# Expert jobs of a top-2-of-8 SwiGLU in plain float32: four column groups of 32 rows on TensorE, weights in rows of 6 and 8 KB in one ring

## The reference

```
def swiglu(x, w_gate, w_up, w_down):
    return (silu(x @ w_gate) * (x @ w_up)) @ w_down

def moe_swiglu(x, w_router, w_gate, w_up, w_down):     # x: 256 x 1024
    logits = xt @ w_router
    top_vals, top_idx = top_k(logits, 2)
    top_w = softmax(top_vals)
    gates = sum(one_hot(top_idx, 8) * top_w)
    for e in range(8):                                  # w_gate[e], w_up[e]: 1024 x 3584, w_down[e]: 3584 x 1024
        out = out + gates[:, e] * swiglu(xt, w_gate[e], w_up[e], w_down[e])
```

## Time and profile before

| what | value |
|---|---|
| time, median of 3 runs | 1460.51 us (1460.16 to 1460.75) |
| profiled execution, first to last instruction | 1458.9 us |
| median less that span | 1.6 us |
| first expert matmul | 495.2 us into the span |
| last expert matmul of weights | 1447.5 us |
| PE, DVE, ACT busy | 99%, 78%, 66% of the span |

### The profile page before, as it was taken

One profiled execution on the slowest core, in us unless ns is written; L12 is line 12 of the kernel. 1 busy time (PEld: TensorE's weight loads), 2 busy tenths in 40 slices (PEclk: granted clock), 3 DMA queues, 4 the chain that ended last, 5 costly groups with the idle time before them and its releaser, 6 DMA issues.

```text
span 1458.9 us, 19214 instructions
## 1 busy us (share of the span) xinstructions
PE 1442.7 (99%) x6982; PEld 1189.6 (82%) x6982; DVE 1142.1 (78%) x841; ACT 970.2 (66%) x820; POOL 110.0 (8%) x186
## 2 busy tenths in 40 slices
PE   9999999999999999999999999999999999999998
PEld 7857888888998888888888888888888888888886
DVE  5756445545555798989898899989898999888997
ACT  5445444334566677777787787787777778777775
POOL 3002000001000540010010010010001001000001
PEclk9999999999999999999999999999999999999999
DMA  8709555553643599999999999999999999999995
GB/s 263 273 1 331 196 179 173 197 192 115 217 145 116 183 382 384 362 394 383 364 383 394 363 371 397 369 362 399 383 353 388 388 369 376 392 371 364 383 380 189
DMA packets 177458, 445.88 MB, mean 306 GB/s; under 512 B 8770, under 2 KB 19074, under 8 KB 161284
## 3 DMA queue, kind: packets, MB, share of 16 engines
q1 hardware_dynamic: 173440, 431.56, 81.4%
q0 software_dynamic: 3968, 13.69, 2.7%
q10 hardware_dynamic: 4, 0.01, 0.0%
HBM read 437.33 MB, written 7.90 MB: 305 GB/s over the span
## 4 chain that ended last, share of the span: by engine, by line
PE 91%; DVE 3%; ACT 3%; issue 2%; DMA 0%; ACTq 0%; POOL 0%; DVEq 0%
PE psum L485 27%; PE psum L487 27%; PE psum L486 27%; PE psum L608 2%; PE psum L1070 2%; ACT w_hi L1252 2%; DVE w_lo L1670 1%; PE psum L444 1%; PE psum L467 1%; PE psum L797 0%; PE psum L788 0%; PE psum L474 0%; PE psum L721 0%; PE psum L1102 0%; PE psum L855 0%
## 5 line engine op out<-in xcount | busy, mean ns | idle before, releaser
L1670 DVE TENSOR_TENSOR w_lo<-raw,w_hi 128x2048 fp32r<-128x2048 f32 x378 | 861.9, 2292 | 180.2 <-ACT w_hi L1252 179.0
L1252 ACT ACTIVATE w_hi<-raw 128x2048 fp32r<-128x2048 f32 x378 | 724.6, 1919 | 270.4 <-PE psum L487 270.3
L485 PE MATMUL psum<-w_hi,x_hi 128*128 128x512 f32 (+2 forms) x1216 | 476.7, 392 | 2.9 <-DVE w_lo L1670 2.6
L487 PE MATMUL psum<-w_hi,x_lo 128*128 128x512 f32 (+2 forms) x1216 | 470.0, 386 | 0.0
L486 PE MATMUL psum<-w_lo,x_hi 128*128 128x512 f32 (+2 forms) x1216 | 469.3, 386 | 0.0
L485 PEld LDWEIGHTS psum<-w_hi,x_hi 128*128 128x128 f32 x1216 | 228.4, 188 | 50.2 <-DVE w_lo L1670 5.5
L487 PEld LDWEIGHTS psum<-w_hi,x_lo 128*128 128x128 f32 x1216 | 228.3, 188 | 46.1
L486 PEld LDWEIGHTS psum<-w_lo,x_hi 128*128 128x128 f32 x1216 | 228.7, 188 | 43.0
L485 PE MATMUL psum<-w_hi,h_hi 128*128 128x512 f32 x576 | 225.3, 391 | 0.0
L487 PE MATMUL psum<-w_hi,h_lo 128*128 128x512 f32 x576 | 224.2, 389 | 0.0
L486 PE MATMUL psum<-w_lo,h_hi 128*128 128x512 f32 x576 | 224.1, 389 | 0.0
(11 more groups left out here) (276 smaller groups left out, 971.8 us busy)
## 6 DMA issues: line engine op xcount, KB each, us to landing
raw<-in_l_w_gate SPq DMA_DIRECT2D x126, 1024.0 KB, 7.3
raw<-in_l_w_up SPq DMA_DIRECT2D x126, 1024.0 KB, 7.6
raw<-in_l_w_down SPq DMA_DIRECT2D x126, 1024.0 KB, 7.2
raw<-in_l_w_in SPq DMA_DIRECT2D x10, 1024.0 KB, 6.4
raw<-in_l_w_out SPq DMA_DIRECT2D x8, 1024.0 KB, 5.9
raw<-in_l_w_in SPq DMA_DIRECT2D x6, 768.0 KB, 14.2
raw<-in_l_w_mem_kv SPq DMA_DIRECT2D x4, 1024.0 KB, 5.9
ys<-xn SPq DMA_DIRECT2D x4, 512.0 KB, 8.5
```

Source lines behind the costliest of these rows:

```text
L485: pe.matmul(out, x[0], w[0], start=first, stop=False, skip_group_check=True)
L487: return pe.matmul(out, x[1], w[0], start=False, stop=last, skip_group_check=True)
L1252: act.activation(w_hi[:, m % CUT, :], raw[:, n % RAW, :], ACT.Copy).then_inc(hi_ok, 1)
L1670: dve.tensor_tensor(w_lo[:, m % CUT, :], raw[:, n % RAW, :], w_hi[:, m % CUT, :].bitcast(F32), ALU.subtract).then_inc(lo_ok, 1)
```

## The change

- `CAP` goes from 128 to 96 rows; the tables allow 13 jobs instead of 11, and an expert may have up to two further jobs. DVE's and POOL's few table instructions of the router stage change with it.
- The expert jobs use no high and low parts. `cut_high`, `cut_rest`, `thrice` and the transposes of the hidden block are gone from the jobs. Every product is a plain float32 matmul.
- Gate and up work on blocks of 1536 and 2048 inner columns. For each k of 8 and each group g of 32 picked rows (three groups), four matmuls have the same 128 x 32 stationary operand, and each writes one quarter of the block's columns (384 or 512) to its own 32 partitions of bank g (gate) or 3 + g (up).
- ACT applies Silu to a whole block in one instruction, DVE multiplies a whole block in one and turns it by one DVE transpose (in blocks of 32 x 32).
- The down product takes 28 chunks of 128 inner rows; two chunks have 12 matmuls of 32 stationary and 512 moving columns, in three sets of four: bank 6 has row groups 0, 1, 2 of the left output half and group 0 of the right, bank 7 groups 1 and 2 of the right half, the even and the odd chunk in different partitions. ACT and DVE put these together afterwards.
- The weights are loaded in 46 pieces: gate and up pieces are one k each (rows of 6 or 8 KB, 768 KB or 1 MB), down pieces 1 MB in rows of 8 KB. They go through a ring of 112 KB a partition, a third of a job, which lies over `raw`, `w_hi`, `w_lo`, `x_hi` and `x_lo`. PE counts a piece as `eaten` with its last matmul, and SP waits for that alone.
- Job 0's pieces in the first 48 KB wait for the slots of `raw`, the rest for the last product of layer 1's output projection. PE begins the jobs once all banks are drained and both halves of the picked rows are copied.
- In the last job the output is first put together in `y_sb` and then cut into the two parts that the tail needs.

```diff
-CAP = P
-MAX_JOBS = NE + NE // 2 - 1
+CAP = 96
+MAX_OVER = 2 * S // (CAP + 1)
+MAX_JOBS = NE + MAX_OVER
...
-TURN = (1, 1, 4, 4, 4, 4, 0, 7)
-USED_TURN = 27
+G = 32
+NGRP = CAP // G
+QUAD = P // G
+FB_E = (1536, 2048)
+FF_E = (0, 1536)
+RING = 28672
...
+        ring = sb("ring", [P, RING])
...
+        act_e = memb[:, :, :].rearrange("p t d -> p (t d)")
+        hid_e = work[:, 0:1536]
+        y_low = work[:, 1536:2048]
+        turned_e = [reg_a[:, 0:NGRP * FB_E[0] // QUAD], reg_b[:, 0:NGRP * FB_E[1] // QUAD]]
+        picked = reg_a[:, 1152:1152 + KD * CAP].rearrange("p (k s) -> p k s", k=KD)
...
+            def source(self, e):
+
+                lo, hi = FF_E[self.blk], FF_E[self.blk] + FB_E[self.blk]
+                if self.kind == "d":
+                    c = FB_E[self.blk] // P
+                    rows_of = t["l1_w_down"][bass.ds(e, 1), lo:hi, :].rearrange("e (p c) n -> p (e c) n", c=c)
+                    return rows_of[:, 2 * self.i:2 * self.i + 2, :]
+                w = t["l1_w_gate" if self.kind == "g" else "l1_w_up"]
+                return w[bass.ds(e, 1), self.i * P:(self.i + 1) * P, lo:hi].rearrange("e p n -> p e n")
...
+        job_pieces = []
+        ring_at = 0
+        for kind, blk in (("g", 0), ("u", 0), ("g", 1), ("u", 1), ("d", 0), ("d", 1)):
+            for i in range(FB_E[blk] // P // 2 if kind == "d" else KD):
+                width = 2 * D if kind == "d" else FB_E[blk]
+                job_pieces.append(Piece(kind, blk, i, ring_at, width))
+                ring_at = (ring_at + width) % RING
+        assert ring_at == 0
+        NJP = len(job_pieces)
+        piece_at = {(x.kind, x.blk, x.i): m for m, x in enumerate(job_pieces)}
+        under = []
+        for m, x in enumerate(job_pieces):
+            older = [n for n in range(m - NJP, m)
+                     if job_pieces[n].at < x.at + x.width and x.at < job_pieces[n].at + job_pieces[n].width]
+            under.append(max(older))
...
+            for b in range(8):
+                pe.wait_ge(drained[b], bk.count[b])
...
-                def expert_rows(kind, b):
-                    label = (kind, b)
-                    bb = 2 + 2 * (b % 2) + (kind == "u")
-                    jbegin(label, bb)
-                    for half in range(2):
-                        if (kind, b) == ("g", 0):
-                            gathered(half)
-                        m = place[kind, b, half]
-                        w = jcut(m, kind)
-                        for c in range(4):
-                            k = 4 * half + c
-                            ins = thrice(bank(bb), (picked_hi[:, k, :], picked_lo[:, k, :]),
-                                         [y[:, c, :] for y in w], k == 0, k == KD - 1)
-                        if half == 0:
-                            use(ins, m)
-                    end(ins, label)
-                    job_free[m] = label
...
+                def landed(kind, blk, i):
+                    x = job_pieces[piece_at[kind, blk, i]]
+                    pe.wait_ge(x.landed, 16 * j + 16)
+                    return x.tile
+
+                def expert_cols(kind, blk):
+
+                    w = FB_E[blk] // QUAD
+                    b0 = 0 if kind == "g" else NGRP
+                    for k in range(KD):
+                        x = landed(kind, blk, k)
+                        for g in range(NGRP):
+                            for c in range(QUAD):
+                                ins = pe.matmul(psum[G * c:G * c + G, b0 + g, 0:w], picked[:, k, G * g:G * g + G],
+                                                x[:, w * c:w * c + w], start=(k == 0), stop=(k == KD - 1),
+                                                skip_group_check=True)
+                        ins.then_inc(eaten, 1)
...
+                def expert_down(blk):
+
+                    pe.wait_ge(turned_ok, 2 * j + blk + 1)
+                    h = turned_e[blk].rearrange("p (g c s) -> p g c s", g=NGRP, s=G)
+                    n = FB_E[blk] // P // 2
+                    for i in range(n):
+                        x = landed("d", blk, i).rearrange("p (c n) -> p c n", c=2)
+                        first, final = blk == 0 and i == 0, blk == 1 and i == n - 1
                         for c in range(2):
-                            cc = 2 * half + c
-                            h = [y[:, b % 2, cc * P:(cc + 1) * P] for y in (h_hi, h_lo)]
-                            ins = thrice(bank(hf), h, [y[:, c, hf * 512:(hf + 1) * 512] for y in w],
-                                         b == 0 and cc == 0, b == NB - 1 and cc == CB - 1)
-                        if b == NB - 1 and half == 1:
-                            end(ins, ("y", hf))
-                    if b == NB - 1 and half == 1:
-                        job_free[m] = ("y", 1)
-                    else:
-                        use(ins, m)
+                            for q, (hf, g) in enumerate(((0, 0), (0, 1), (0, 2), (1, 0))):
+                                pe.matmul(psum[G * q:G * q + G, 6, :], h[:, g, 2 * i + c, :],
+                                          x[:, c, hf * 512:(hf + 1) * 512], start=(first and c == 0),
+                                          stop=(final and c == 1), skip_group_check=True)
+                        for q, (g, c) in enumerate(((1, 0), (2, 0), (1, 1), (2, 1))):
+                            ins = pe.matmul(psum[G * q:G * q + G, 7, :], h[:, g, 2 * i + c, :], x[:, c, 512:1024],
+                                            start=first, stop=final, skip_group_check=True)
+                        ins.then_inc(eaten, 1)
...
+                pe.wait_ge(picked_ok, j + 1)
+                expert_cols("g", 0)
+                expert_cols("u", 0)
+                pe.wait_ge(gate_out, 2 * j + 1)
+                expert_cols("g", 1)
+                pe.wait_ge(up_out, 2 * j + 1)
+                expert_cols("u", 1)
+                pe.wait_ge(y_out, j + 1)
+                pe.wait_ge(y_mid, j + 1)
+                expert_down(0)
+                if last:
+                    turn_last()
+                else:
+                    next_rows()
+                expert_down(1)
...
+                def gate(blk):
+                    w = FB_E[blk] // QUAD
+                    act.wait_ge(eaten, NJP * j + piece_at["g", blk, KD - 1] + 1)
+                    if blk == 1:
+                        act.wait_ge(up_out, 2 * j + 1)
+                    act.activation(act_e[:, 0:NGRP * w].rearrange("p (g c) -> p g c", g=NGRP),
+                                   psum[:, 0:NGRP, 0:w], ACT.Silu).then_inc(gate_out, 1)
+
+                gate(0)
+                gate(1)
...
+                act.wait_ge(eaten, NJP * j + NJP)
+                act.activation(y_low[G:2 * G, :], psum[2 * G:3 * G, 7, :], ACT.Copy)
+                act.activation(y_low[2 * G:3 * G, :], psum[3 * G:4 * G, 7, :], ACT.Copy)
+                act.activation(y_sb[0:G, 512:1024], psum[3 * G:4 * G, 6, :], ACT.Copy).then_inc(y_low_ok, 1)
+                act.activation(y_sb[0:CAP, 0:512], psum[0:CAP, 6, :], ACT.Copy,
+                               scale=gate_of[0:CAP, bass.ds(j, 1)]).then_inc(y_out, 1)
+                if last:
+                    act.wait_ge(y_out, j + 2)
+                    for hf in range(2):
+                        if hf == 1:
+                            act.wait_ge(y_rows, j + 1)
+                        cs = slice(hf * 512, (hf + 1) * 512)
+                        act.activation(y_parts[0][0:CAP, cs], y_sb[0:CAP, cs], ACT.Copy).then_inc(y_hi_ok, 1)
...
+                def hidden(blk):
+                    w = FB_E[blk] // QUAD
+                    x = hid_e[:, 0:NGRP * w]
+                    if blk == 1:
+                        dve.wait_ge(turned_ok, 2 * j + 1)
+                    dve.wait_ge(gate_out, 2 * j + blk + 1)
+                    dve.wait_ge(eaten, NJP * j + piece_at["u", blk, KD - 1] + 1)
+                    dve.tensor_tensor(x.rearrange("p (g c r) -> p g c r", g=NGRP, r=G),
+                                      act_e[:, 0:NGRP * w].rearrange("p (g r c) -> p g c r", g=NGRP, r=G),
+                                      psum[:, NGRP:2 * NGRP, 0:w].rearrange("p g (r c) -> p g c r", r=G),
+                                      ALU.mult).then_inc(up_out, 1)
+                    dve.wait_ge(up_out, 2 * j + blk + 1)
+                    dve.transpose(turned_e[blk], x).then_inc(turned_ok, 1)
+
+                hidden(0)
+                hidden(1)
...
+                for g in (1, 2):
+                    ins = dve.tensor_tensor(y_sb[G * g:G * g + G, 512:1024], psum[G * (g - 1):G * g, 7, :],
+                                            y_low[G * g:G * g + G, :], ALU.add)
+                ins.then_inc(y_mid, 1)
+                dve.wait_ge(y_mid, j + 2)
+                dve.tensor_scalar(y_sb[0:CAP, 512:1024], y_sb[0:CAP, 512:1024], gate_of[0:CAP, bass.ds(j, 1)], None,
+                                  ALU.mult).then_inc(y_rows, 1)
+                if last:
+                    for hf in range(2):
```

(70 more changed lines are left out.)

374 lines of the change are left out of this document (121 added, 253 removed).

## The result

The changed kernel takes 1425.95 us (median of 4 executions, 1422.8 to 1428.97) against 1460.34 us: a ratio of 0.9767, with a 95% interval of 0.9751 to 0.9783. That is 34.4 us less; 72 less were forecast. 1426 is inside the range of 1374 to 1439. The profiled execution took 1422.8 us, with a span of 1420.6.

The account below looks back on a forecast made before the run. The prediction took PE's own matmuls to bound the jobs. It summed 495.2 us before the jobs, 8 x 109.5 - 0.8 for them, the 16.1 us tail and 1.6 us around the span to 1388.1 us, range 1374 to 1439.

Parts of the forecast that it names:

- The loop's code must be fetched again each time: Rival at PE's loop return: code is refetched at each of seven returns, 0 to 51 us in all; chance 0.07.
- PE's matmuls: In the jobs: four column quarters run at once, so a job's sets take 108.2 us.
- The 1.3 us for transposes and emptying: On PE in a job: 0.8 us for the next rows' eight transposes, 0.5 us for emptying and filling around them.
- The first rival: In the jobs' sets: quarters overlap only in part; with two streams a job is 217.7 us, the kernel 2254; chance 0.20.
- Start and tail: Before the jobs: no change, within 1 us, jobs from 495.2 us; after them: tail grows from 11.1 to 16.1 us.
- Loads at nothing: Weight loads beside the jobs: at 405 GB/s the last piece lands at 1346.6 us, so they add 0 us.
- ACT and DVE at nothing: In the jobs: removed cuts save nothing; Silu, multiply, DVE transposes and output work lie beside PE's matmuls, adding 0 us.
- The number of jobs: Expert jobs stay eight, as the largest count is 90; an expert over 96 would add a ninth, 109.5 us.

Follow-up runs that it names:

- quarter_loads: The changed kernel, with each load from the second expert on bringing only a quarter of its columns, the other weights left out: 1397.97 us, ratio 0.9571.
- the written-out kernel: The changed kernel with PE's jobs written out eight times and no loop on PE, all else as it is: 1387.78 us, ratio 0.9496.
- the body of 1443 records: The changed kernel with a shorter PE loop: some sets of four gate and up matmuls became single ones, those products left out: 1395.09 us.

## Why the prediction was right, and where it wasn't

**The step that failed** is the term for the loop's return, which the sum has at nothing: the chance, and with it the price, given to *The loop's code must be fetched again each time*. The count that it rests on was right (2208 against 1080), the trace had the silence of the old loop's instruction queue, and the rival's price of 0 to 51 us holds what came, 6 x 6 = 36 us. (It counts seven returns; there are six.) Yet it had 0.07, and the forecast put 0 us. In its place the runs showed 5.8 us a return, 4.3 of idle time and some 1.5 of lost work at half clock, 35 us in all. The row at hand for the price was the loads' issue to landing, 7.3 us. The branch in fact lasts 5.8 to 6.7 us, close to that ceiling; what brings the idle time down to 4.3 is the 2.1 us of matmuls that PE starts meanwhile, an overlap that the prediction didn't look for. What nobody could read from the rows of before is the half clock behind the hole. The prediction gives no reason for a chance as low as 0.07; what it has is the silence of the old loop's queue, and that says only that the loop before was held. It says nothing of a loop twice as long.

**PE's matmuls.** Right. Four quarters run at once: job 0 takes 108.9 us with its transposes, where the sum has 108.2 for the sets alone, and 109.15 us is measured without returns, against 109.5. The 1.3 us for transposes and emptying was 0.3 too much. The first rival, which had one chance in five, is excluded by the same windows. The ratio of 2.38 for three column tiles on the Trainium skill's page TensorE: Matmul & The Clock Gate (Part 3, measured speedup) isn't seen in this stream: by the prediction's estimate from it a job would take 137.8 us.

**Start and tail.** The first expert matmul stands at 494.9 us (495.2 forecast). The last weight matmul starts at 1404.07 us and ends 0.43 later, so the tail is 1420.6 - 1404.5 = 16.1 us, as forecast. In the sum, 494.9 + 108.9 + 6 x 115.3 + 108.7 + 16.1 = 1420.4 us, and the span is 1420.6.

**Loads at nothing.** Right: PE never waits for a transfer in the changed kernel's jobs, and the rate at hand is higher than any row of before (417 GB/s against 404 and 405). It was closer than the text had it: at 417 the loads need 108.5 us of the 109.15. Through the fetch the loads did matter after all: 2.8 us of each return come from the wait of the code's packet behind them.

**ACT and DVE at nothing.** Right: 7.1 and 10.0 us of a job, 6 and 9%, and no wait of PE for them in the jobs.

**The number of jobs** stayed eight.

## What to carry to other kernels

When a change makes a hardware loop's body longer, count the instructions of the engine that sets the end. Here a PE loop of up to 1587 records turned for 0.3 to 0.7 us a pass more than written-out code, and from 1659 on each return cost 6 us. Where exactly the limit lies for a loop that begins elsewhere was not measured. Where the trips are few and known, write them out: the code then arrives ahead of its use and costs nothing. In this kernel that is worth 38 us (1425.95 to 1387.78), or 32 with the general case kept behind a jump. A queue that is silent in the trace of before shows what fits, not how much room is left.

## What the runs showed of the hardware

- A PE loop of up to 1587 records between branches ran without fetches; one of 1659 fetched all of its code in each pass. The Trainium skill's page Runtime: NRT & Kernel Launch (Instruction fetch mechanics) gives PE 2048 instructions; the measurement is lower, by a fifth.
- The price of a taken branch to code that isn't held: the branch lasts 3.4 to 3.8 us with loads at 107 GB/s and 5.8 to 6.7 us at 394, of which 1.5 and 4.3 us are idle time of PE, against 0.21 to 0.25 us where the code is held. The Trainium skill's page Runtime: NRT & Kernel Launch (Instruction fetch mechanics) says that a taken branch whose target isn't in the current window of two blocks of 16 KB waits for a fetch. The runs agree on the wait, but not on that window: by the same section's 256 instructions to 16 KB it would be 512, and loops of 1148 to 1587 records were held. That the fetch stands in line with the data is what the runs add.
- In the changed kernel the granted clock fell to 1.2 GHz at five of six holes of 4 us, for 3.4 us, once for 6.8; at the holes of quarter_loads, 1.1 to 2.0 us from start to start, it never did. It is low elsewhere too: in the profile of the written-out kernel it is at 0.50 between 484.6 and 494.8 us, in the router stage, and the jobs begin at 499.2 us instead of 495.0. That is a spread of some 4 us between executions which no edit made (the profile of the body of 1443 records has it too).
- Four plain float32 matmuls of 32 stationary columns, each with its own moving stream, ran fully at once: 138 sets and 8 transposes took 109.15 us, where a single quarter of the columns would need 108.2 by the 0.430 us of a record of 512 columns.
